# Running the experts of a mixture layer as four couples, a full job and a half-size job with two weight passes

## The reference

```python
def moe_ffn(xn, router_w, router_b, w1, w3, w2):
    logits = (xn @ router_w).astype(jnp.float32) + router_b.astype(jnp.float32)
    top_v, top_i = lax.top_k(logits, TOP_K)
    w = jax.nn.softmax(top_v, axis=-1)
    gate = jnp.sum(jax.nn.one_hot(top_i, N_EXPERTS, dtype=jnp.float32) * w[..., None], axis=-2)
    out = jnp.zeros_like(xn)
    for e in range(N_EXPERTS):
        out = out + gate[..., e:e + 1] * swiglu(xn, w1[e], w3[e], w2[e])
    return out
```

## Time and profile before

| | us |
|---|---|
| median of three runs | 1931.6 |
| the profiled execution, own time | 1931.0 |
| its span, first to last instruction | 1929.2 |
| mixture stage, first weight matmul to the end of the passed extra jobs | 869.7 to 1886.9 |
| TensorE busy over the span | 1814.0 (94%) |
| VectorE / ScalarE busy | 1506.8 (78%) / 1215.1 (63%) |

### The profile page before, as it was taken

How to read it: one execution, slowest core, us unless ns; L and a number is a source line. 1 busy time by engine, 2 the same in 40 slices (tenths; PEclk the granted TensorE clock), 3 DMA queues, 4 the chain that set the end, 5 groups by cost and what they waited for, 6 DMA issues and landing times. The chain is left out here.

```text
span 1929.2 us, 29647 instructions
## 1 busy us (share of the span) xinstructions
PE 1814.0 (94%) x10818; PEld 1587.2 (82%) x10819; DVE 1506.8 (78%) x2092; ACT 1215.1 (63%) x1664; POOL 2.4 (0%) x15
## 2 busy tenths in 40 slices
PE   4988899999998889889999999999999999999987
PEld 4766899999996768887888888888888888888877
DVE  6685686656678774958889889889898888988965
ACT  4545744433455548346778777778777777877754
POOL 0000000000000000000000000000000000000000
PEclk9999999999999999999999999999999999999998
DMA  7422263645534323527989989989899898998951
GB/s 272 149 99 99 107 221 127 239 155 201 196 128 174 104 88 127 198 92 290 383 330 357 379 306 381 358 322 381 307 376 379 310 381 327 360 378 306 382 226 67
DMA packets 36788, 485.38 MB, mean 252 GB/s; under 512 B 4048, under 2 KB 6368, under 8 KB 7136
## 3 DMA queue, kind: packets, MB, share of 16 engines
q1 hardware_dynamic: 34416, 481.96, 65.4%
q10 hardware_dynamic: 2288, 2.28, 0.4%
HBM read 483.15 MB, written 1.07 MB: 251 GB/s over the span
## 5 line engine op out<-in xcount | busy, mean ns | idle before, releaser
L1754 DVE TENSOR_TENSOR w_lo<-raw,w_hi 128x1024 fp32r<-128x1024 f32 x672 | 776.0, 1218 | 85.2 <-ACT w_hi L812 84.9
L812 ACT ACTIVATE w_hi<-raw 128x1024 fp32r<-128x1024 f32 x672 | 668.4, 1055 | 103.2 <-DMA raw<-in_moe_w 53.8
L464 DVE TENSOR_TENSOR w_lo<-raw,w_hi 128x1024 fp32r<-128x1024 f32 x236 | 283.2, 1221 | 165.1 <-ACT w_hi L459 162.8
L919 PE MATMUL work<-w_hi,bias_r 128*128 128x512 f32 x896 | 356.3, 398 | 3.7 <-DVE bias_r L1739 3.7
L921 PE MATMUL work<-w_hi,bias_r 128*128 128x512 f32 x896 | 350.3, 391 | 0.0
L920 PE MATMUL work<-w_lo,bias_r 128*128 128x512 f32 x896 | 349.7, 390 | 0.0
L919 PE MATMUL work<-x_r,w_hi 128*128 128x256 f32 x1024 | 300.8, 294 | 15.0 <-DVE w_lo L464 10.8
L920 PE MATMUL work<-x_r,w_hi 128*128 128x256 f32 x1024 | 292.4, 286 | 0.0
L921 PE MATMUL work<-x_r,w_lo 128*128 128x256 f32 x1024 | 292.2, 285 | 0.0
L459 ACT ACTIVATE w_hi<-raw 128x1024 fp32r<-128x1024 f32 x236 | 240.6, 1047 | 61.5 <-PE work L921 29.0
L919 PEld LDWEIGHTS work<-x_r,w_hi 128*128 128x128 f32 x1024 | 199.2, 194 | 23.5 <-issue 17.8
(11 more groups left out here) (302 smaller groups left out, 2384.9 us busy)
## 6 DMA issues: line engine op xcount, KB each, us to landing
raw<-in_moe_w SPq DMA_DIRECT2D x168, 2048.0 KB, 9.7
raw<-in_mix_w SPq DMA_DIRECT2D x34, 2048.0 KB, 8.2
raw<-in_dense_w SPq DMA_DIRECT2D x21, 2048.0 KB, 8.2
raw<-in_ple_w SPq DMA_DIRECT2D x4, 2048.0 KB, 10.1
areaK<-in_ple_p SPq DMA_DIRECT2D x2, 1024.0 KB, 10.0
hT<-in_xT SPq DMA_DIRECT2D x1, 1024.0 KB, 5.4
gate_b<-bias_line ACTq DMA_DIRECT2D x1, 1024.0 KB, 8.2
areaB<-bias_line ACTq DMA_DIRECT2D x1, 1024.0 KB, 10.6
```

What stands on the lines that cost most here:

```text
L464: eng.tensor_tensor(unit(w_lo, g), raw_part(g), unit(w_hi, g).bitcast(F32), ALU.subtract).then_inc(split_ok, 1)
L812: act.activation(w_hi[u][:, :], raw[n % RING][:, (i % 4) * QUARTER:(i % 4 + 1) * QUARTER], ACT.Copy).then_inc(hi_ok, 1)
L919: pe.matmul(out, stat[0], move[0], start=start, stop=False, skip_group_check=True)
L1754: dve.tensor_tensor(w_lo[u][:, :], raw[n % RING][:, (i % 4) * QUARTER:(i % 4 + 1) * QUARTER], w_hi[u][:, :].bitcast(F32), ALU.subtract).th ...
```

## The change

Experts are sorted by load on the chip and run as four couples. The first job of a couple (heavy) takes up to 128 tokens and is computed as before. The second (light) takes up to 64 tokens. Its gather puts the same 64 tokens twice side by side, the first half is replaced by its rounded high part and the second by the remainder, and this one stationary operand goes past w_hi and w_lo: two passes in place of three (`stacked_product`). The two halves of the result are added when it is transposed: `fold` is a 128x64 matrix of two identities, and the transposes become ordinary float32 matmuls by it, one set for each of the two hidden pieces, before silu and product. Expert 0 is always the first heavy job, since its first twelve quarters are loaded before the order is known; the four least loaded of the other seven are light. A light expert with over 64 tokens, or a heavy one with over 128, gets a full extra job, up to four. Every weight quarter is its own DMA (512 KB, 128 partitions by 4 KB), waits for the quarter twelve before it, and has the arrival semaphore of its slot quarter. `order_experts` on DVE, of which the diff shows the start, goes on with ten more small operations on tables of up to 128 columns, nearly all followed by a settle (a wait for the operation's own end). `light_plain()` returns the empty set, so that all quarters are split in light jobs too (LIGHT_Q is 84).

```diff
-EXTRA = (2 * T) // (P + 1)
+COUPLES = EXPERTS // 2
+LIGHT = P // 2
+EXTRA = 4
...
+            def load_part(e, kind, where, i, g):
+                if g < 4 * RING:
+                    ge(sp, split_ok, kind, where, i, JOB_Q, LIGHT_Q, MOE_Q - 4 * RING + g + 1)
...
+                else:
+                    ge(sp, split_ok, kind, where, i, JOB_Q, LIGHT_Q, MOE_Q + SPLIT_AT[kind].index(g - 4 * RING) + 1)
+                src = moe_w[e, g // 4][:, (g % 4) * QUARTER:(g % 4 + 1) * QUARTER]
+                sp.dma_start(raw_quarter(g), src).then_inc(part_full[part_slot(g)], 16)
...
-                    with sp.Fori(0, EXPERTS) as e:
-                        load_expert(e, e, 0)
+                    for g in range(4 * RING):
+                        sp.wait_ge(split_ok, before_moe[g // 4])
+                        sp.dma_start(raw_quarter(g), moe_w[0, g // 4][:, (g % 4) * QUARTER:(g % 4 + 1) * QUARTER]).then_inc(part_full[part_slot(g)], 16)
+                    sp.wait_ge(sorted_ok, 1)
+                    with sp.Fori(0, COUPLES - 1) as i:
+                        e = expert_of(bass.ds(i * 2, 1))
+                        for g in range(4 * RING, JOB_Q):
+                            load_part(e, "heavy", "couple", i, g)
+                        e = expert_of(bass.ds(i * 2 + 1, 1))
+                        for g in range(JOB_Q):
+                            load_part(e, "light", "couple", i, g)
...
@@ act
+                def light_gate_taken(c):
+                    act.activation(l_a, work[0][:, :], ACT.Copy).then_inc(m_silu_ok, 1)
+                def light_lin_taken(c):
+                    act.activation(l_b, work[1][:, :], ACT.Copy).then_inc(l_b_taken, 1)
+                def light_silu(c):
+                    act.activation(l_gate, folded(pv_ps), ACT.Silu).then_inc(l_silu_ok, 1)
+                def light_hi(c):
+                    act.activation(hidT_hi[:, :, 0:LIGHT], l_hid, ACT.Copy).then_inc(l_hi_ok, 1)
...
@@ pe
+                def stacked_product(out, stat, move, start, stop):
+                    pe.matmul(out, stat, move[0], start=start, stop=False, skip_group_check=True)
+                    return pe.matmul(out, stat, move[1], start=False, stop=stop, skip_group_check=True)
...
+                def turn_light_gate(c):
+                    for ft in range(FT):
+                        mm = pe.matmul(folded(pv_ps)[:, ft, :], l_a[:, ft * P:(ft + 1) * P], fold, start=True, stop=True)
+                def turn_light_lin(c):
+                    for ft in range(FT):
+                        mm = pe.matmul(folded(misc)[:, ft, :], l_b[:, ft * P:(ft + 1) * P], fold, start=True, stop=True)
...
+                    elif light:
+                        if c == FC:
+                            pass
+                        else:
+                            turn_light_lin(c - 1)
...
+                    if light and c < FC:
+                        turn_light_gate(c)
+                    if light and c == FC:
+                        turn_light_lin(c - 1)
...
@@ dve
+            def order_experts(rank, gate):
+                for n, p in enumerate((0, 1, 5, 2, 6, 3, 7, 4)):
+                    step(dve.memset(place_of[:, n:n + 1], float(p)))
+                    step(dve.memset(cap[:, n:n + 1], float((P, LIGHT)[n % 2])))
+                step(dve.tensor_scalar(ids, pick_w, -1.0, float(EXPERTS), ALU.mult, ALU.add))
+                step.settle()
+                step(dve.scalar_tensor_tensor(out=key, in0=count, scalar=float(EXPERTS), in1=ids, op0=ALU.mult, op1=ALU.add))
+                step.settle()
+                step(dve.memset(key[:, 0:1], -1.0))
+                step.settle()
+                step(dve.tensor_tensor(by_job, over_jobs(key), over_experts(key), ALU.is_lt))
+                step.settle()
...
-                    if i == 2:
-                        split_gathered(j + first)
-                    lo_m(i)
+                    if g == 2:
+                        split_gathered(kind, where, i)
+                    if g in SPLIT_AT[kind]:
+                        lo_m(g)
+                        else:
+                            if g == M_TURN[c] + AHEAD:
+                                light_hidden(c)
+                            if g == M_TURN[c] + AHEAD + (1 if c < FC - 1 else 0):
+                                light_lo(c)
...
+                with dve.Fori(0, COUPLES) as i:
+                    job("heavy", "couple", i)
+                    job("light", "couple", i)
```

More of the change, by code:

```diff
@@ L155, in trunk @@
     MIX_AT = {"qkv": 0, "lx": 3, "gb": 5, "ga": 7, "pa": 9, "lg": 11, "pb": 13, "out": 15}
+    PLAIN = {"heavy": set(), "light": light_plain()}
+    SPLIT_AT = {kind: [i for i in range(JOB_Q) if i not in PLAIN[kind]] for kind in PLAIN}
+    LIGHT_Q = len(SPLIT_AT["light"])
     quarters = []
@@ L803, in job @@
[L803 to L813, removed]
+                    ge(act, m_gathered, kind, where, i, 2, 2, half + 1)
@@ L872, in moe @@
                     with act.Else():
-                        job(r, EXPERTS)
-                take_y(JOBS)
+                        job("heavy", "extra", r)
+                take_y("heavy", "extra", EXTRA)
                 hi.n = phase_q[(l, "ple")]
@@ L1149, in ple, with gather @@
                         norm_root(n)
[L1151 to L1153 removed]
+            def gather(kind, where, i, more):
+                ge(pe, m_built, kind, where, i, 1, 1, more + 1)
                 for half in range(2):
@@ L1175, in combine, with job, part @@
                     mm.then_inc(m_combined, 1)
[L1177 to L1181, removed]
+            def job(kind, where, i):
+                light = kind == "light"
+                def part(g, k):
+                    ge(pe, split_ok, kind, where, i, JOB_Q, LIGHT_Q, MOE_Q + SPLIT_AT[kind].index(g) + 1)
+                    u = part_unit(kind, g)
@@ L1188, in up @@
-                    if c:
-                        pe.wait_ge((m_silu_ok, m_hid_ok)[half], j * FC + (first * FC + c))
-                    for q in range(4):
[L1192 to L1196, removed]
+                        ge(pe, m_xg, kind, where, i, 2, 2, 2)
@@ L1223, in job @@
                     if c == 0:
-                        combine(j + first)
+                        combine(kind, where, i)
+                    elif light:
+                        if c == FC:
+                            pass
+                        else:
+                            turn_light_lin(c - 1)
                     else:
@@ L1279, in moe @@
                 pe.sem_inc(part_used, UNITS_HELD)
-                gather(0)
-                with pe.Fori(0, EXPERTS) as e:
-                    job(e, 0)
+                gather("heavy", "couple", 0, 0)
+                pe.wait_ge(fold_ok, 1)
+                with pe.Fori(0, COUPLES) as i:
+                    job("heavy", "couple", i)
+                    job("light", "couple", i)
                 pe.wait_ge(extra_ok, 1)
@@ L1289, in moe @@
                     with pe.Else():
-                        job(r, EXPERTS)
-                combine(JOBS)
+                        job("heavy", "extra", r)
+                combine("heavy", "extra", EXTRA)
             pe.wait_ge(consts, 2)
@@ L1796, in moe @@
                 dve.sem_inc(m_gtaken, 1)
+                dve.tensor_tensor(fold, ident[:, 0:LIGHT], ident[:, LIGHT:P], ALU.add).then_inc(fold_ok, 1)
+                norm_root(3 * l + 1)
+                routing()
                 extra_jobs()
-                with dve.Fori(0, EXPERTS) as e:
-                    job(e, 0)
+                with dve.Fori(0, COUPLES) as i:
+                    job("heavy", "couple", i)
+                    job("light", "couple", i)
                 with dve.Fori(0, EXTRA) as r:
```

429 lines of the change are left out of this document (289 added, 140 removed).

## The result

| | us |
|---|---|
| before, median (1931.19 to 1931.96) | 1931.6 |
| changed, median of four (1893.46 to 1898.14) | 1893.9 |
| ratio, 95% interval | 0.9815 [0.9803, 0.9827] |
| forecast and range | 1888, 1861 to 1924 |

The account below looks back on a forecast made before the run. Transfers at 373 GB/s were to end each couple, 239 us against 250.7. From the profiled 1931.0 us: 46.8 saved, 2.4 added at the start, 1.0 at the end, 0.6 for the median: 1888 us, range 1861 to 1924.

Parts of the forecast that it names:

- Dropped passes: TensorE in a light job: one pass in three goes, 38.2 us less, bringing its need from 125.3 to 97 us.
- VectorE in a light job: All 84 quarters still split, sixteen operations narrower: 105.5 us of work plus 1.5 of waits, 107 us.
- The transfers: Weight loads in the mixture: 88.1 MB a couple at 373 GB/s takes 236 us, narrowly ending it over computing's 232.3.
- The signs that I had named: Mixture stage: DMA share 0.97 or more at 365 to 380 GB/s, light-job TensorE near 85% busy, ScalarE waiting for raw.
- Rival A: Mixture transfers hold 385 GB/s or more, computing ends a couple at 232 to 233 us: 1863 us; chance 0.12.
- rival C: Small quarter transfers don't stream, 329 GB/s, a couple takes 268 us: 2003 us, slower; chance 0.12.
- The couple: Heavy plus light job: 236 us by transfers plus 3 for stock edges, 239 against 250.7, four times 11.7 saved.
- The start: Sorting on VectorE before the first split delays TensorE's first matmul: +2.4 us, bounds +1.5 to +5.
- The end: Before the last combine four extra jobs are passed in place of three: +1 us, 0 to +3.
- B: Light job's hand-overs before `down` cost 1.5 us more a chunk, light job 118 us: kernel 1915 us; chance 0.10.
- D: Idle spells hold TensorE at 1.2 GHz in light jobs, 183 us each: kernel 2150 us; chance 0.02.
- E: Expert 5's load of 64 overflows the light limit, adding a full job of 125 us: 2013 us; chance 0.02.

Follow-up runs that it names:

- half splits: Light jobs of the written-out version make w_lo for only the left half of each weight quarter: 1855.4 us, ratio 0.9611.
- Written out: Changed kernel with the couples as plain code in place of a hardware loop on TensorE, ScalarE and VectorE, SP's loop kept: 1874.8 us, ratio 0.9718.
- ScalarE written out: Changed kernel with the couples' hardware loop replaced by plain code on ScalarE alone, TensorE and VectorE keeping theirs: 1893.6 us, ratio 0.9813.

## Why the prediction was right

The time came out right. The bound that the forecast named did not: it let the transfers end a couple, and VectorE does.

**Dropped passes.** Right, and shown by the run with three passes: 135.05 us where the forecast's terms add to 135.

**VectorE in a light job.** Forecast 107 us (105.5 busy and 1.5 of waits), measured 109.8, with VectorE busy 103.0 and idle 6.8. The term was 3 us short, and by its waits: the waits view has 5.7 us for w_hi alone where I allowed 1.5 for all hand-overs; for instance ScalarE, in order, waits for VectorE's product before it rounds it.

**The transfers.** This step failed. The forecast let them end a couple, at 373 GB/s and 236.2 us against 232.3 for computing. Halving them in light jobs took only 3.9 us off the kernel (1870.9 against 1874.8). The price itself was nearly right: where half splits let the transfers end the couple, its 88.1 MB took 230.9 us, 382 GB/s, 5 us less than forecast. The cost of a row held as well: the median packet of 4 KB took 159 ns in the trace of the changed kernel (162 worked out), one of 16 KB 611 ns (615). What was wrong is the order of two sums only 4 us apart. Written out, the couple takes 235.8 us because VectorE's side is that long (111 and 124.6); that this is the forecast's 236.2 is luck. The signs that I had named could not tell the two apart: light jobs had the share of 0.97 at 371 GB/s, as forecast, without being ended by the transfers. The sign that did tell was ScalarE waiting for raw, and it did not come (0.9 us).

Rival A had the mechanism, computing ends the couple; it had the price too low, since it kept 107 for the light job and had no border. The limit of 358 GB/s that the Trainium skill gives (page DMA: Bandwidth & Descriptors, section Specifications) did not bind here: 409 GB/s in the last 40 us of a light job and 384 over a heavy one (half splits) stand above it. Its rule of at least 1 MiB a DMA (section Rules for kernel authors), named beside rival C, doesn't hold for this flow either: at 512 KB, with transfers queued, the share was 1.00 at 379 GB/s. The fit that the prediction takes from section Anatomy of one DMA is given there for DMAs that GpSimd issues; SP issues these, and no run here shows a lone quarter.

**The couple.** 239 us forecast, and 0.6 for the start spread over four; 242.4 is the mean of the four measured, start included. The forecast had 3 us for stock and edges and nothing for the loop. The jump cost 8 us in each of three heavy jobs, 24 us by the difference to the written-out version, of which 19 show in the ratios. It wasn't in any step. The loop's own jumps took 0.2 us before, but the same trace has one dear jump, 6.7 us on TensorE's queue where the first extra job is passed (L1287), and the forecast didn't ask what makes it dear. That the sum came out within 6 us is in part a cancelling of errors: 3 us a couple for edges that did not show, and nothing for a border that cost 6 us a couple.

**The start.** From the first gather to the first matmul before took 9.1 us (860.57 to 869.65), after 12.4 (859.09 to 871.54): 3.4 us for the 2.4 forecast (whose sorting term adds up to 3.1 us, not 3.2). Sorting took 4.0 us, for its operations on 64 and 128 columns run 0.26 to 0.32 us apart, not 0.20. Two rows show it:

```profile
861.76 0.22 DVE L1866 TENSOR_REDUCE gate_a<-gate_a 128x8 f32<-128x64 f32 x1
862.02 0.22 DVE L1868 TENSOR_TENSOR gate_a<-gate_a 128x64 f32<-128x64 f32 x1
```

**The end.** Forecast +1 us. TensorE's idle fell instead, 12.81 to 10.28 us with four passed jobs. Its first jump to the passing branch took 3.3 us, not 6.7, which would account for it; no run tests that:

```profile
1848.26 2.07 PE L1292 MATMUL pv_ps<-gate_b,spare 128*128 128x256 f32 x4 [10.28 <-ACT spare L898]
```

**Rivals.** B (a chained light job) is true to 3 us, not to 11. C, D and E didn't come: no light load overflowed, and between the start and the last job the half clock stands only after the 6.5 us at borders. D's price has a slip: with 183 us for a light job a couple is 308 and the kernel about 2165, not 2150. The chances of the rivals that end slower (C, D and E) add up to 0.16, not 0.14.

The sum by place, from gathers: the eight jobs -34.5 us (forecast -44.4 with the start), what lies ahead of them -1.5 and behind -0.7 (forecast 0 and +1; why the stretch ahead is shorter I didn't trace); together -36.7, as the spans have it (1929.2 to 1892.5).

## What to carry to other kernels

Price a job that is freed of its first bound by the next two, not only by the next: here they stood 5 and 11 us behind, and a high DMA share alone didn't say which of them ends. Ask with whom the others wait, and take the transfers away to be sure. When the body of a hardware loop grows, look at its jump back as at a wait on every engine at once, and ask how much queued work lies over it on the engine that ends last.

## What the runs showed of the hardware that I had not expected

The jump back of a loop took 0.2 us with one job in the body and 5.2 to 6.2 us with two, on a kernel otherwise the same; ScalarE stood 3.6 to 5.1 us at it, and VectorE 5.4 with ScalarE written out. With 8.2 us of work queued on TensorE when ScalarE stopped, 1.5 to 2.0 us of idle were left; with 4.5 us queued, 6.6. Where between one and two jobs it sets in wasn't tried.

Transfers of 512 KB with 4 KB rows reached 409 GB/s in the last 40 us of a light job, and 370 at a share of 0.99 earlier in the same job. A share near 1 is not a fixed rate. The queue was deeper in the faster stretch. The DMA view of the two stretches, the faster first (count, KB each, median us from issue to landing):

```profile
raw<-in_moe_w SPq DMA_DIRECT2D x33, 512.0 KB, 11.6
```

```profile
raw<-in_moe_w SPq DMA_DIRECT2D x16, 512.0 KB, 7.2
```

With one issue every 1.2 us that makes about ten transfers under way in the first and six in the second, an estimate from these rows. That the depth is what made the difference is not shown.
